# Dilated attention in two query layouts with maxima of their own, in three passes instead of one loop

## What is computed

```python
DIL_PATTERNS = ((128, 1), (512, 4), (2048, 16))   # (window, dilation)
# dilated_group: per residue class of the positions modulo dil
dist = qi + BLK - kj
valid = (dist >= 0) & (dist <= steps) & (blk * BLK + kj - BLK >= 0)   # steps = 128
s = jnp.where(valid, s, NEG); m = max(s); p = exp(s - m); den = sum(p)
o = p @ v / den;  lse = m + log(den)
# dilated_mixer: the three patterns are joined
wts = softmax(stack(lses));  o = sum(stack(outs) * wts)
# memory_attention, 4 heads, 256 keys, unmasked
p = softmax(q @ k.T * hd ** -0.5);  o = p @ v
```

## Time and profile before

| what | value |
|---|---|
| time, median of 3 runs (range) | 3669.84 us (3669.31 to 3673.82) |
| profiled execution: its time | 3668.56 us |
| its span | 3667.2 us |
| first transpose of the values (start of the part) | 3154.84 us |
| first product of the output projection (its end) | 3260.48 us |
| PE busy over the span | 94% |

### The profile page before, as it was taken

One profiled execution on the slowest core, in us unless ns is written; L12 is line 12 of the kernel. 1 busy time (PEld: TensorE's weight loads), 2 busy tenths in 40 slices (PEclk: granted clock), 3 DMA queues, 4 the chain that ended last, 5 costly groups with the idle time before them and its releaser, 6 DMA issues. The chain is left out here.

```text
span 3667.2 us, 42469 instructions
## 1 busy us (share of the span) xinstructions
PE 3450.9 (94%) x15384; PEld 2691.5 (73%) x15384; DVE 1806.8 (49%) x1934; ACT 719.8 (20%) x1404; POOL 2417.9 (66%) x1113
## 2 busy tenths in 40 slices
PE   7999998999998999999899998987999999779998
PEld 6888765688876888775678886654788877558886
DVE  5453435454647545244464474687454224355521
ACT  2110123311113111103421112214311100231100
POOL 7888741488876888773178886660488777328875
PEclk9999998999999999998899999987999999899999
DMA  3233220122331223221022332220122232102232
GB/s 117 97 100 103 86 69 24 58 93 96 112 120 58 92 97 102 91 92 46 18 88 96 105 104 92 92 69 1 64 98 97 98 120 87 41 29 96 95 100 94
DMA packets 84366, 305.98 MB, mean 83 GB/s; under 512 B 9360, under 2 KB 9616, under 8 KB 83856
## 3 DMA queue, kind: packets, MB, share of 16 engines
q1 hardware_dynamic: 80928, 292.59, 23.7%
q10 hardware_dynamic: 3312, 11.71, 0.9%
HBM read 300.07 MB, written 4.19 MB: 83 GB/s over the span
## 5 line engine op out<-in xcount | busy, mean ns | idle before, releaser
L469 POOL TENSOR_TENSOR WH<-raw,zero 128x1024 fp32r<-128x1024 f32 (+1 forms) x554 | 1047.6, 1891 | 1180.1 <-DMA raw<-in_w 1086.2
L471 POOL TENSOR_TENSOR WL<-raw,WH 128x1024 fp32r<-128x1024 f32 (+1 forms) x554 | 1372.1, 2477 | 43.5
L539 PE MATMUL psA<-HH,WH 128*128 128x512 f32 x1216 | 484.5, 398 | 2.4 <-DVE PROJ L1509 2.4
L541 PE MATMUL psA<-HL,WH 128*128 128x512 f32 x1216 | 475.5, 391 | 0.0
L540 PE MATMUL psA<-HH,WL 128*128 128x512 f32 x1216 | 475.4, 391 | 0.0
L541 PE MATMUL psC<-HIDL,WH 128*128 128x512 f32 x1056 | 417.1, 395 | 0.0
L539 PE MATMUL psC<-HIDH,WH 128*128 128x512 f32 x1056 | 417.1, 395 | 0.0
L540 PE MATMUL psC<-HIDH,WL 128*128 128x512 f32 x1056 | 417.1, 395 | 0.0
L539 PE MATMUL psC<-HH,WH 128*128 128x512 f32 x800 | 313.4, 392 | 3.8 <-DVE HL L1410 3.8
L1338 DVE TENSOR_TENSOR HIDL<-Y,HIDH 128x512 f32 (+1 forms) x132 | 254.2, 1925 | 126.7 <-ACT HIDH L1060 126.7
L541 PE MATMUL psC<-HL,WH 128*128 128x512 f32 x800 | 311.6, 389 | 0.0
(11 more groups left out here) (274 smaller groups left out, 4889.9 us busy)
## 6 DMA issues: line engine op xcount, KB each, us to landing
raw<-in_w SPq DMA_DIRECT2D x554, 512.0 KB, 3.3
X<-in_x ACTq DMA_DIRECT2D x4, 512.0 KB, 8.9
NRAW<-in_mem ACTq DMA_DIRECT2D x2, 1024.0 KB, 5.5
out<-Y SPq DMA_DIRECT2D x8, 256.0 KB, 2.1
POSI<-in_pos ACTq DMA_DIRECT2D x4, 256.0 KB, 3.5
PRAW<-in_p ACTq DMA_DIRECT2D x2, 512.0 KB, 5.1
table_F<-newF ACTq DMA_DIRECT2D x2, 512.0 KB, 5.0
table_I<-newI ACTq DMA_DIRECT2D x2, 512.0 KB, 7.6
```

The lines of the kernel that those rows point to most:

```text
L469: pool.tensor_tensor(WH[j][:, 0:w], raw[j][:, 0:w], zero[:, 0:1].broadcast_to([P, w]), ALU.subtract).then_inc(w_hi, 1)
L471: pool.tensor_tensor(WL[j][:, 0:w], raw[j][:, 0:w], WH[j][:, 0:w], ALU.subtract).then_inc(w_split, 1)
L539: pe.matmul(out, WH[slot][:, w], hi[:, t], start=start and t == 0, stop=False)
L541: mm = pe.matmul(out, WH[slot][:, w], lo[:, t], start=False, stop=stop and t == tiles - 1)
```

## The change

The near pattern gets a query layout of its own: 128 consecutive tokens (block layout), so that it needs 256 keys (128 for b = 0) and a mask that is the same for all b. The other two patterns keep every fourth token (step layout). A row is then 512 scores in one bank, a pair half of psA and psB. Since the two halves of a row now belong to different queries, each has its own maximum and sum, and both have to be joined before the weights are known. The one loop becomes passes:

1. `dil_scores` on PE, `dil_peaks` on DVE, `dil_exponentials` on ACT: scores of all 8 pairs, two in flight, all exponentials kept (`PR` and a second buffer `PR2`). One piece of the values' transposition stands behind each pair.
2. `attend("mem_dil")`, with its own buffer `PRM`. Inside of it DVE spreads maxima and sums over columns (`dil_spread`, 8 instructions), PE permutes their partitions with two products (`dil_exchange`), DVE gathers them (`dil_gather`, 8 and 3), ACT takes an exponential and DVE forms the factors (`dil_factors`, 5). The first scores also wait now for the exponentials of the pass before.
3. `dil_weigh`: DVE multiplies the factors in, 4 instructions a pair (`dil_normalize`), PE turns into four banks (psC, psA) and weighs two pairs behind; ACT copies.

The first of these four are what PE's first transposes of the third pass wait for. The core of the diff:

```diff
-    band_raw = sb("band_raw", [P, NBAND], offset=ar + 48 * KB)
-    band = sb("band", [P, NBAND], BF16, offset=ar + 44 * KB)
+    exch = sb("exch", [P, NE], offset=ar + 44 * KB)
+    ST = sb("ST", [P, 2, 2, 4 * QB], offset=ar + 44 * KB + 1088)
+    XT = sb("XT", [P, 2, 2, 4 * QB], offset=ar + 44 * KB + 1344)
+    XD = sb("XD", [P, 2, 2, 4 * QB], offset=ar + 44 * KB + 1600)
+    XM = sb("XM", [P, 2, QB, 2 * 4 * QB], offset=ar + 44 * KB + 1856)
+    XN = sb("XN", [P, 2, 4 * QB], offset=ar + 44 * KB + 2880)
+    XF = sb("XF", [P, 2, 4 * QB], offset=ar + 44 * KB + 3008)
...
+    PR2 = sb("PR2", [P, 8 * S], offset=HLo)
+    PRM = sb("PRM", [P, 8 * MEM], offset=SQo)
...
+    DIL_PAIRS = [(c, b) for c in range(2) for b in range(QB)]
+    dil_bank = lambda j, x: (PA, PB)[j % 2][:, x]
+    dil_first = lambda b: 0 if b > 0 else P
+    dil_stat = lambda c, b, x: (2 * c + x) * QB + b
+    dil_part = lambda b, g: slice(dil_first(b), 2 * P) if g == 0 else slice(2 * P, S)
+    def dil_probs(j, x):
+        i = 2 * j + x
+        return (PR, PR2)[i // 8][:, i % 8 * S:(i % 8 + 1) * S]
+    def dil_turns(j):
+        b = DIL_PAIRS[j][1]
+        return [(x, k) for x in range(2) for k in range(0 if b > 0 else 1, 4)]
+    def dil_values(c, b, x, k):
+        hc = slice((2 * c + x) * HD, (2 * c + x + 1) * HD)
+        return (VT[:, 0, b - 1 + k, hc], slice(b * P, (b + 1) * P)) if k < 2 else (VT[:, k - 1, b, hc], slice(b, S, QB))
+    dil_turned_at = lambda j, i: (j % 4 * 8 + i) * P
+    dil_turn_bank = lambda t: (PC, PA)[t % 4 // 2][:, t % 2]
...
+        def dil_scores():
+            pe.wait_ge(rot_done, n.now(rot_done))
+            pe.wait_ge(pj_done, n.now(pj_done))
+            base = n.now(p_exp)
+            tokens = v_list("mem_dil") + v_list("dil")
+            for j, (c, b) in enumerate(DIL_PAIRS):
+                if j >= 2:
+                    pe.wait_ge(p_exp, base + 2 * (j - 2) + 2)
+                rows = [slice(0, 64), slice(64, 128)]
+                near = slice(b * P - P if b > 0 else 0, (b + 1) * P)
+                for x, r in enumerate(rows):
+                    pe.matmul(dil_bank(j, x)[:, dil_first(b):2 * P], PROJ[r, c, b * P:(b + 1) * P], PROJ[r, 2 + c, near],
+                              start=True, stop=False, skip_group_check=True)
+                for g in (1, 2):
+                    for x, r in enumerate(rows):
+                        pe.matmul(dil_bank(j, x)[:, (1 + g) * P:(2 + g) * P], PROJ[r, 6 * g + c, b::QB], PROJ[r, 6 * g + 2 + c, b::QB],
+                                  start=False, stop=False, skip_group_check=True)
+                for x in range(2):
+                    pe.matmul(dil_bank(j, x)[:, dil_first(b):2 * P], identb[:], mb[:, M_BAND + dil_first(b):M_CAUSAL + P],
+                              start=False, stop=True, skip_group_check=True)
+                    mm = pe.matmul(dil_bank(j, x)[:, 2 * P:S], identb[:], mb[:, M_CAUSAL:M_DIL16 + P],
+                                   start=False, stop=True, skip_group_check=True)
+                mm.then_inc(s_ready, 1)
+                to_token(tokens[j], j)
+            n.full(p_exp, 2 * len(DIL_PAIRS))
+        def dil_exchange():
+            pe.wait_ge(xm_ready, n.full(xm_ready))
+            for layout, at in ((0, E_TO_STEP), (1, E_TO_BLOCK)):
+                mm = pe.matmul(MS_X[:, layout * P:(layout + 1) * P], exch[:, at:at + P], XM[:, layout].rearrange("p r n -> p (r n)"),
+                               start=layout == 0, stop=layout == 1, skip_group_check=True)
+            mm.then_inc(x_got, 1)
+        def dil_weigh():
+            base, out_base = n.now(pt_done), n.now(ol_ready)
+            turns, weighed = 0, 0
+            for j in range(len(DIL_PAIRS) + 2):
+                if j < len(DIL_PAIRS):
+                    blocks = dil_turns(j)
+                    pe.wait_ge(p_norm, n.full(p_norm, 2))
+                    for g, m in groups(len(blocks)):
+                        pe.wait_ge(pt_done, base + max(turns - 3, 0))
+                        for i, (x, k) in enumerate(blocks[g:g + m]):
+                            t = pe.transpose(dil_turn_bank(turns)[:, i * P:(i + 1) * P], dil_probs(j, x)[:, k * P:(k + 1) * P], ident)
+                        t.then_inc(pt_ready, 1)
+                        turns += 1
+                if j >= 2:
+                    c, b = DIL_PAIRS[j - 2]
+                    blocks = dil_turns(j - 2)
+                    if j == 2:
+                        pe.wait_ge(ol_ready, out_base)
+                    weighed += len(groups(len(blocks)))
+                    pe.wait_ge(pt_done, base + weighed)
+                    for i in sorted(range(len(blocks)), key=lambda i: (blocks[i][1], blocks[i][0])):
+                        x, k = blocks[i]
+                        v, cols = dil_values(c, b, x, k)
+                        at = dil_turned_at(j - 2, i)
+                        mm = pe.matmul(PD[64 * x:64 * x + 64, c, cols], v, PRT["dil"][:, at:at + P], start=b == 0 and k == 1,
+                                       stop=b == QB - 1 and k == 3, skip_group_check=True)
+                    mm.then_inc(pv_done, 1)
+            n.room(pt_done, turns)
+            n.full(ol_ready, 2)
...
-                to_tokens("mem_dil")
-                to_tokens("dil")
-                attend("dil")
+                dil_scores()
                 attend("mem_dil")
+                dil_weigh()
...
+        def dil_exponentials():
+            tokens = v_list("mem_dil") + v_list("dil")
+            for j, (c, b) in enumerate(DIL_PAIRS):
+                act.wait_ge(nm_ready, n.full(nm_ready))
+                for x in range(2):
+                    at = dil_stat(c, b, x)
+                    for g in range(2):
+                        part = dil_part(b, g)
+                        ins = act.activation(dil_probs(j, x)[:, part], dil_bank(j, x)[:, part], ACT.Exp, bias=ST[:, g, 0, at:at + 1],
+                                             accum_out=ST[:, g, 1, at:at + 1])
+                    ins.then_inc(p_exp, 1)
+                to_token(tokens[j], j)
+        def dil_exchange():
+            act.wait_ge(xd_ready, n.full(xd_ready))
+            act.activation(XD[:], XD[:], ACT.Exp).then_inc(xe_ready, 1)
+        def dil_weigh():
+            used_base, turns = n.now(pv_done), 0
+            for j in range(len(DIL_PAIRS) + 2):
+                if j < len(DIL_PAIRS):
+                    if j >= 4:
+                        act.wait_ge(pv_done, used_base + j - 3)
+                    for g, m in groups(len(dil_turns(j))):
+                        at = dil_turned_at(j, g)
+                        act.wait_ge(pt_ready, n.full(pt_ready))
+                        act.activation(PRT["dil"][:, at:at + m * P], dil_turn_bank(turns)[:, 0:m * P], ACT.Copy).then_inc(pt_done, 1)
+                        turns += 1
+                if j >= 2 and (j - 1) % 4 == 0:
+                    c = (j - 2) // 4
+                    act.wait_ge(pv_done, used_base + j - 1)
+                    act.activation(OH["dil"][:, c], PD[:, c], ACT.Copy).then_inc(oh_ready, 1)
+            n.full(pv_done, len(DIL_PAIRS))
...
+                if which == "mem_dil" and j in (1, 2, 4):
+                    (dil_spread, dil_gather, dil_factors)[(1, 2, 4).index(j)]()
...
+        def dil_peaks():
+            for j, (c, b) in enumerate(DIL_PAIRS):
+                both = ST[:, :, 0].rearrange("p g (h b) -> p h g b", b=QB)[:, 2 * c:2 * c + 2, :, b:b + 1]
+                banks = (PA, PB)[j % 2][:, :, :].rearrange("p x (g n) -> p x g n", g=2)
+                dve.wait_ge(s_ready, n.full(s_ready))
+                if b > 0:
+                    dve.tensor_reduce(both, banks, AX.X, ALU.max, negate=True).then_inc(nm_ready, 1)
+                else:
+                    dve.tensor_reduce(both[:, :, 0], banks[:, :, 0, P:2 * P], AX.X, ALU.max, negate=True)
+                    dve.tensor_reduce(both[:, :, 1], banks[:, :, 1], AX.X, ALU.max, negate=True).then_inc(nm_ready, 1)
+        def dil_spread():
+            dve.wait_ge(p_exp, n.full(p_exp, 2 * len(DIL_PAIRS)))
+            for layout, col in ((0, E_STEP), (1, E_BLOCK)):
+                for i in range(QB):
+                    ins = dve.tensor_scalar(XM[:, layout, i], ST[:, layout].rearrange("p k n -> p (k n)"), exch[:, col + i:col + i + 1],
+                                            None, ALU.mult)
+            ins.then_inc(xm_ready, 1)
+        def dil_gather():
+            dve.wait_ge(x_got, n.full(x_got))
+            for layout, src, col in ((1, MS_X[:, 0:P], E_BLOCK), (0, MS_X[:, P:2 * P], E_STEP)):
+                got = src.rearrange("p (a k h n) -> p a k h n", a=QB, k=2, h=4)
+                out = XT[:, layout].rearrange("p k (h a) -> p a k h", a=QB)
+                for i in range(QB):
+                    one = exch[:, col + i:col + i + 1]
+                    if i == 0:
+                        ins = dve.tensor_scalar(out, got[:, :, :, :, i], one, None, ALU.mult)
+                    else:
```

(59 more changed lines are left out.)

92 lines of the change are left out of this document (36 added, 56 removed).

## The result

The changed kernel takes 3621.3 us (3619.4 to 3622.6, 4 runs) against 3670.5 (3669.3 to 3673.8) for the kernel before beside it: 49.2 us less, ratio 0.9858, 95% interval 0.9845 to 0.9872. The prediction was 3636 with 3626 to 3656, a gain of 34 us.

What follows compares the result with a forecast made beforehand. PE was taken to bound the kernel outside attention, a ring of mutual waits the dilated loop. 21.4 + 4.0 + 25.0 + 21.5 = 71.9 us in place of 105.6, 33.7 less, gave 3636 us, range 3626 to 3656.

Steps and rivals of the forecast that it cites:

- What else moves: Outside the attention part: the cast of `band`, ACT's smaller load, DMA timing and POOL's weight ring change nothing.
- pass one, to the end of the last masks: Dilated scores, masks and turning of values, two pairs in flight, at full clock: 21.4 us, including 0.5 added.
- wait behind it: Before the memory rows' first scores, which wait for ACT's last copy of values: 4.0 us, nothing covers it.
- memory rows with the exchange: Memory rows at 20.3 us as now, some 3.5 for the exchange, 1.2 for lower clock: 25.0 us.
- weighing, with the gap ahead and the chain behind: Third pass, PE-bound: 1.0 multiplying, 16.2 transposes, products and changes, 0.3 start, 2.5 half clock, 1.5 end: 21.5 us.
- the ring of the earlier trace: Old dilated loop: every engine waits for another, since one pair holds both score buffers; ACT 42.2, DVE 38.6, PE 19.3 us.
- The half clock behind the gap: Start of the third pass, after about 3 us without work for PE: 2.5 us added.
- that of a full pass, 0.27: Tiling changes on PE: the skill's drain rule read as a full array pass, near 2.2 us instead of 1.3, time 3637.
- Half clock in the first pass: Rival: PE stays at half clock in the passes, 7.6 us gained, 3662; all of it 3%, half (3649) 10%.
- The dear exchange: Rival, memory rows: 24 small instructions at 0.69 us instead of 0.19, 12 us more, 3648; chance 11%.
- No overlap: Rival, first pass: pairs go through PE, DVE, ACT in turn, 48 us instead of 21, 3663; chance 3%.
- Slower: Rival: the 24 small instructions eat the whole gain, from 1.6 us each; with 1.8 each 3675; chance 3%.

Runs made afterwards that it cites:

- the traces with the later clock: Changed kernel with one pair in flight (3641.4 us) and with the first two pairs multiplied ahead of the last low part (3622.9 us); full clock returned later.

## Why the prediction was wrong

**The step that failed** is the one that begins "What else moves". It went through DMAs, the cast and the ring of weights, and answered "nothing" to each. It did not ask where the tiles lie. The diff has both halves of the cause, `NM = 4 * P` and `scalars`, with all large tiles allocated behind them. The missing term is six times 2.33, 14.0 us, from the traces of before and after. The address alone, timed, gave 3672.9 - 3657.4 = 15.5 us. Without this miss the time would have been inside the range: the part's own error, 3.1 us, leads to 3633. With the missing term the prediction would have been about 3622; that this meets the 3621.3 is partly luck, since the part came out 3.1 us shorter than forecast and the rest of the program some 3 us longer (below).

**The sum of the part** held to 3.1 us:

| term | predicted | measured |
|---|---|---|
| pass one, to the end of the last masks | 21.4 | 20.6 |
| wait behind it | 4.0 | 3.8 |
| memory rows with the exchange | 25.0 | 24.9 |
| weighing, with the gap ahead and the chain behind | 21.5 | 19.4 |
| part | 71.9 | 68.8 |

Pass one: the first masks of the third and fourth pair start 2.73 us apart (2.8 was the forecast). The waits tell that PE and the softmax keep the same pace, as the prediction had it; in the first pass, who for whom, us, times, longest:

```profile
DVE ST L1636 <- PE psB L817: 6.4, 4, 1.9
...
ACT PR L1207 <- DVE ST L1636: 2.4, 5, 0.9
...
PEld psB L808 <- ACT PR L1207: 1.3, 3, 0.5
```

Of the ring of the earlier trace rows, in which ACT waited 42.2 us for the maxima, 2.4 are left here. The wait behind the pass and the gap ahead of the third pass came out as chains of the same links, with PE idle for 3.3 us (3.5 to 4 was the forecast) and 2.3 us (2.5):

```profile
3173.61 1.22 PE L877 MATMUL psA<-KVM,PROJ 64*128 64x256 f32 x4 [3.34 <-ACT VT L1197]
...
3199.45 0.88 PE L841 MATMUL psC<-cf,PR 128*128 128x128 f32 x6 [2.34 <-DVE PR L1683]
3200.50 1.92 PE L841 MATMUL psA<-cf,PR 128*128 128x128 f32 x8 [0.17 <-DVE PR L1683]
```

Memory rows: the right sum with offsetting sizes. The small instructions are dearer than I took them; DVE in 3170 to 3190, busy, mean ns:

```profile
L1661 DVE SCALAR_TENSOR_TENSOR XT<-psD,exch,XT 128x32 f32<-128x32 f32 x6 | 1.6, 274 | 0.2
L1646 DVE TENSOR_SCALAR XM<-ST,exch 128x32 f32<-128x32 f32 x8 | 1.3, 237 | 0.0
...
L1672 DVE TENSOR_TENSOR XF<-XD,XT 128x32 f32<-128x32 f32 x1 | 0.2, 194 | 0.0
```

Eight spreading instructions took 1.25 us (1.0), the gathering with its three 3.0 (2.4), the factors 1.3 (1.1), 5.5 together instead of 4.5. But PE's two products were ready when DVE came for them, which saved the 0.6 us. Taking all of it away gave back 4.0 us, or 5.6 against the traces with the later clock; the forecast's 4.7 lies between, and no trace here settles it closer.

Weighing: the last term, mis-sized by 2.1 us. The half clock behind the gap was taken at 2.5 us. The second row of transposes (3200.50) took 1.92 us against 1.09 at full clock, and two such rows are most of it; behind the same gap, at full clock, the kernel without the exchange was 1.5 us shorter. The 1.3 us for changes between transposes and products were counted beside durations that already held part of them. The third pass at full clock:

```profile
3208.74 1.09 PE L841 MATMUL psA<-cf,PR 128*128 128x128 f32 x8
3209.76 1.09 PE L855 MATMUL psD<-PRTb,VT 128*64 128x128 f32 x16
3210.79 1.09 PE L841 MATMUL psC<-cf,PR 128*128 128x128 f32 x8
3211.81 0.88 PE L855 MATMUL psD<-PRTb,VT 128*64 128x128 f32 x12
```

A pair takes 2.05 us, where the terms give 2.14 with the change. Inside a row transposes start 0.109 us apart and products, two records each, 0.109 too. By these a pair would take 1.75, so 0.3 us go to its two changes, 0.15 for each. The price of the row, 0.16 us a change, was right, then, and that of a full pass, 0.27, was too high. The Trainium skill's rule that the engine drains at such a change (TensorEngine Tiling (Array Packing), Key Properties) fits as far as the trace shows that a change costs PE time.

**The rivals.** Half clock in the first pass: not there (1.00), though the experiment with one pair in flight shows how near it is (0.66 where PE waits up to 2.8 us for each pair). The dear exchange: 0.24 us a small instruction, nearer to 0.19 than to 0.69. No overlap: refuted by the trace, and its price, 24 us, was near the 27 of the prediction. Slower: the small instructions are far from 1.6 us.

**What the sums leave.** 36.9 and 14.0 make 50.9, and the spans differ by 47.9. The 3 us between lie in the rest of the program, in stretches with pauses for PE, where the same code takes different times from run to run. The 96 products of the output projection behind the part, in the changed kernel and in the one with the region moved down, which starts them 10.5 us earlier:

```profile
3217.90:3245.20 27.30, 23.61 (x95) 18.69 (x96) 20.71 (x16) 7.47 (x12) 14.13 (x6) 0.94 0.18 59
```

```profile
3207.40:3231.60 24.20, 22.44 (x96) 17.96 (x97) 17.69 (x15) 7.47 (x12) 13.97 (x6) 1.00 0.21 66
```

Of the 3.1 us between them 1.9 are pauses in which PE waits for DVE's `X` (L1442), and 1.2 are products at half clock behind the longer one. DVE was busy for 20.7 us here and 17.7 there with nearly the same work: some of its instructions take longer while POOL is splitting weights. One of them, in the changed kernel and then in the one with the region moved down, where it starts just ahead of POOL:

```profile
3227.04 1.90 POOL L483 TENSOR_TENSOR WH<-raw,scalars 128x1024 fp32r<-128x1024 f32 x1 [65.21 <-DMA raw<-in_w]
3227.13 2.35 DVE L1389 SCALAR_TENSOR_TENSOR HL<-X,VALL,HH 128x512 fp32r<-128x512 f32 x1
```

```profile
3216.56 0.75 DVE L1389 SCALAR_TENSOR_TENSOR HL<-X,VALL,HH 128x512 fp32r<-128x512 f32 x1
3216.61 2.44 POOL L483 TENSOR_TENSOR WH<-raw,scalars 128x1024 fp32r<-128x1024 f32 x1 [65.42 <-DMA raw<-in_w]
```

So 0.1 us in when the two engines meet became 1.6 us for one of them, and a pause of PE with a fall of the clock came behind it. Other stretches scatter too: from the fourth to the fifth down projection all eleven kernels run the same code (with five addresses of the region) and took 650.7 to 655.9 us, and the old attention part took 102.5 to 106.8 us in the four traces of it. This is why a single run can't tell 2 us. A trace can, where the clock is the same in both. Between the down projections the changed kernel's trace is 7.5 us longer than that of before up to the fifth, and 4.6 us shorter behind it, the part itself left out; together these are the 3 us. How much of either is DVE beside POOL and how much is clock was not worked out.

## What to carry to other kernels

Where an engine is the bound, an edit that changes the size of a small tile can move every large tile behind it, so compare the addresses of the operands before and after, and look in the trace at the pace of products that the edit doesn't touch. Where engines wait for each other in a ring, try a second item in flight: of 37 us here two thirds hung on it, part of them by TensorE's clock, and one third on shorter items. Count the fixed price of small instructions (0.15 to 0.35 us on DVE here) before moving a reduction into another layout, and put them where another pass keeps PE busy. Before a gain of 2 us is put down to an edit, compare the granted clock of the stretch in both traces.

## What the runs showed of the hardware

- fp32 products of 128x512 with activations in a region whose start has remainder 0 or 64 by 256 bytes ran 0.2333 us apart, with 192 0.2289, and with 128 0.227, the same to 0.01 us in 122 us in all six places. It is 3% of the time of these products, with nothing waiting in any trace.
- DVE on 32 elements: 0.14 us apart without a wait (0.24 long), 0.31 apart for `scalar_tensor_tensor` out of PSUM that waits for the one before.
- DVE beside POOL: `HL<-X,VALL,HH` (L1389 of after, 512 columns, two inputs in SBUF) took 0.74 to 0.75 us in all 48 cases in which POOL was idle, and 1.25 to 2.85 us in the 12 that lay wholly inside POOL's work. `X<-X,psC` (L1442, one input in PSUM) took 0.68 to 0.69 us in all 32 cases, 19 of them wholly inside POOL's work.
- PE going over between 128x128 transposes and 128x64 products: 0.15 us for each change, at full clock.
- PE on half rows (64 of 128) beside each other: in the first pass of after it was busy for 19.6 of 20.7 us with a granted clock of 1.00; with one pair in flight it was busy for 26.3 of 44.2 us with 0.66.
